# Two transformer blocks on one core: small inputs on another queue, rotary angles and row transposes earlier, the gate columns in another stage

## The reference

```
mod = c @ w_ada + b_ada                       # c is one row: 1024 -> 3 x 1024
shift, scale, gate = split(mod, 3)
h = rmsnorm(x, pre_norm_g) * (1 + scale) + shift
q, k, v, z_ret, u_val, u_gate, z_conv, g_a, g_b = split(h @ w_in)
qh, kh = rotary(q, positions), rotary(k, positions)
y_a = (head_groupnorm(retention(qh, kh, v)) * silu(z_ret)) @ w_ret_out
a = silu(layernorm(causal_depthwise_conv(u_val * sigmoid(u_gate), conv_w) + conv_b))
y_b = (a * silu(z_conv)) @ w_conv_out
y = (sigmoid(g_a) * y_a + sigmoid(g_b) * y_b) @ w_out
x = x + gate * rmsnorm(y, post_norm_g)        # gate is wanted here only
```

## Time and profile before

| | |
|---|---|
| median of three runs | 1937.9 us (1937.62 to 1944.29) |
| profiled execution, its own time | 1937.75 us |
| its span | 1935.9 us, so 1.85 us lie around the span |
| PE busy, mean granted clock | 1719.5 us (89%), 0.943 of full speed |
| DVE, ACT, POOL busy | 1138.3, 893.8, 796.3 us |
| DMA | 357.94 MB, mean 185 GB/s |

### The profile page before, as it was taken

How to read it: one execution, slowest core, us unless ns; L and a number is a source line. 1 busy time by engine, 2 the same in 40 slices (tenths; PEclk the granted TensorE clock), 3 DMA queues, 4 the chain that set the end, 5 groups by cost and what they waited for, 6 DMA issues and landing times.

```text
span 1935.9 us, 22760 instructions
## 1 busy us (share of the span) xinstructions
PE 1719.5 (89%) x7364; PEld 1246.5 (64%) x7364; DVE 1138.3 (59%) x1523; ACT 893.8 (46%) x1196; POOL 796.3 (41%) x388
## 2 busy tenths in 40 slices
PE   1888999989999899989689998873999999999993
PEld 1766878777878688458577467662566656666562
DVE  4667865472232346335553314225899998998995
ACT  3534433443224122123321134331888888888882
POOL 0476977333424144104202031100566556665663
PEclk9899999999999899999859999885999999999997
DMA  8344435222242213412104232122999999999995
GB/s 287 115 121 124 129 118 184 88 97 93 76 147 88 109 40 123 165 66 82 67 1 128 87 131 87 44 87 85 337 395 396 393 389 389 396 391 395 389 370 189
DMA packets 138669, 357.94 MB, mean 185 GB/s; under 512 B 12661, under 2 KB 64125, under 8 KB 113768
## 3 DMA queue, kind: packets, MB, share of 16 engines
q1 hardware_dynamic: 130264, 325.32, 46.1%
q10 hardware_dynamic: 4544, 18.88, 2.5%
q0 software_dynamic: 3792, 12.85, 2.1%
HBM read 333.95 MB, written 23.07 MB: 184 GB/s over the span
## 4 chain that ended last, share of the span: by engine, by line
PE 48%; issue 19%; POOL 14%; DVE 11%; DMA 4%; ACT 2%; SPq 1%; POOLq 0%; DVEq 0%; ACTq 0%
PE ps L720 11%; PE ps L721 11%; PE ps L722 11%; PE ps L692 10%; POOL parts L2284 9%; PE ps L702 3%; POOL idx L2294 2%; DMA ring<-in_w_in 1%; DVE act_parts L1671 1%; POOL parts L2250 1%; PE ps L928 1%; PE ps L901 1%; POOL arena L2297 1%; DMA ring<-in_w_out 1%; DMA arena<-in_sgu_b 1%
## 5 line engine op out<-in xcount | busy, mean ns | idle before, releaser
L2250 POOL TENSOR_TENSOR parts<-ring,parts 128x1024 fp32r<-128x1024 f32 x150 | 371.0, 2480 | 808.1 <-ACT parts L1087 805.3
L1366 ACT CAST parts<-ring 128x1024 fp32r<-128x1024 f32 x384 | 396.2, 1048 | 90.9 <-PE ps L722 67.2
L720 PE MATMUL ps<-parts,act_parts 128*128 128x512 f32 (+2 forms) x1088 | 427.8, 393 | 7.1 <-DVE parts L2074 2.2
L721 PE MATMUL ps<-parts,act_parts 128*128 128x512 f32 (+2 forms) x1088 | 423.7, 389 | 0.0
L722 PE MATMUL ps<-parts,act_parts 128*128 128x512 f32 (+2 forms) x1088 | 423.2, 389 | 0.0
L2074 DVE TENSOR_TENSOR parts<-ring,parts 128x1024 fp32r<-128x1024 f32 x289 | 394.3, 1415 | 26.0 <-ACT parts L1366 19.3
L2284 POOL TENSOR_TENSOR parts<-ring,parts 128x1024 fp32r<-128x1024 f32 x95 | 264.1, 2781 | 235.8 <-ACT parts L1366 235.2
L1087 ACT CAST parts<-ring 128x1024 fp32r<-128x1024 f32 x150 | 155.6, 1047 | 409.4 <-PE ps L722 288.5
L720 PE MATMUL ps<-act_parts,parts 128*128 128x512 f32 x640 | 253.9, 397 | 20.4 <-POOL parts L2250 15.6
L721 PE MATMUL ps<-act_parts,parts 128*128 128x512 f32 x640 | 251.0, 392 | 0.0
L722 PE MATMUL ps<-act_parts,parts 128*128 128x512 f32 x640 | 250.9, 392 | 0.0
(11 more groups left out here) (248 smaller groups left out, 1824.3 us busy)
## 6 DMA issues: line engine op xcount, KB each, us to landing
ring<-in_w SPq DMA_DIRECT2D x192, 1024.0 KB, 7.6
ring<-in_w_in SPq DMA_DIRECT2D x30, 1024.0 KB, 7.3
ring<-in_w_in SPq DMA_DIRECT2D x34, 512.0 KB, 5.6
ring<-in_w_ada SPq DMA_DIRECT2D x12, 1024.0 KB, 11.4
ring<-in_w_ret_out SPq DMA_DIRECT2D x8, 1024.0 KB, 10.8
ring<-in_w_out SPq DMA_DIRECT2D x8, 1024.0 KB, 9.7
y_rows<-arena ACTq DMA_DIRECT2D x32, 256.0 KB, 6.4
ring<-in_w_in SPq DMA_DIRECT2D x16, 256.0 KB, 4.0
```

The source lines that it names most:

```text
L720: pe.matmul(o, lhs[1], rhs[0], start=start, stop=False)
L721: pe.matmul(o, lhs[0], rhs[1], start=False, stop=False)
L1366: act.copy(parts[:, n % 4, 0, :], ring[:, j, n % 4 * 1024:(n % 4 + 1) * 1024]).then_inc(piece_hi, 1)
L2250: pool.tensor_tensor(parts[:, g % 4, 1, :], ring[:, st.place(j), k * 1024:(k + 1) * 1024], parts[:, g % 4, 0, :].bitcast(F32), ALU.subtrac ...
```

## The change

It does these things:

- The positions, the small rows and the conv taps are issued by ACT at its very start, from ACT's queue. SP issues all of `ada` 0 to 3 behind x without them.
- The angle work is DVE's first work; it waits for the constants and the positions.
- On PE, `hT` comes ahead of `columns`.
- The gate's chunks leave the conv loop. In the `mix` stage they pass through slots 1 and 2, between chunks 2 and 3 of the mix; DVE sums them behind the merges of the first third; PE adds them up between the two halves of the last third, and DVE multiplies with `post_norm_g` ahead of the last third's merges. SP loads `post_norm_g` and the bias behind mix chunk 3, when `actT_ready` has reached 24. `conv_use` and `conv_chunk` go, `mix_use` comes, the bank and chunk plans follow.

```diff
@@ plans @@
-    ("columns", 1, 1), ("hT", KT, 1), ("mod", 1, 1), ("conv", [CONV_BANKS[k % 6] for k in range(conv_use(5 * KT))], 1), ("hq0", GROUP_A, 1),
+    ("hT", KT, 1), ("columns", 1, 1), ("mod", (1,), 1), ("conv", [CONV_BANKS[(k + 1) % 6] for k in range(5 * KT)], 1), ("hq0", GROUP_A, 1),
...
-    *[(f"mix{n}", GROUP_A + GROUP_B, 1) for n in range(3)],
+    *[(f"mix{n}", GROUP_A + GROUP_B, 1) for n in range(2)], ("mix2", GROUP_A, 1), ("gate", GROUP_B[2:], 1), ("mix2b", GROUP_B, 1),
...
-    ("ada", 4, 1), ("conv", [(k + 1) % 3 for k in range(3 * KT + 2)], 1), ("hq0", 1, 1), *[(f"head{h}", (1, 2, 0), 1) for h in range(HEADS - 1)],
-    (f"head{HEADS - 1}", (1, 2), 1),
-    ("mix", 6, 1), ("out", 2, 1), ("in2", (2, 0, 1, 0), 1),
+    ("ada", 4, 1), ("conv", [(k + 1) % 3 for k in range(3 * KT)], 1), ("hq0", (1,), 1), *[(f"head{h}", (2, 0, 1), 1) for h in range(HEADS - 1)],
+    (f"head{HEADS - 1}", (2, 0), 1),
+    ("mix", (1, 2, 0), 1), ("gate", (1, 2), 1), ("mix_rest", (0, 1, 2), 1), ("out", 2, 1), ("in2", (2, 0, 1, 0), 1),
...
@@ sync: start @@
             ada("ada", 0, 0)
-            per_feature = [a["conv_w"][0], a["conv_b"], a["conv_ln_g"], a["conv_ln_b"], row(a["norm_mix_2"]),
...
-                sp.dma_start(colrows[at:at + v.shape[0], :], v).then_inc(cols_in, 16)
...
-            sp.dma_start(sgub_rows[:, :], a["sgu_b_2"]).then_inc(cols_in, 16)
             ada("ada", 1, 1)
             ada("ada", 2, 2)
             ada("ada", 3, 3)
-            sp.dma_start(pos_i[:, :], a["positions"].partition_broadcast(P)).then_inc(pos_in, 16)
@@ sync: conv loop @@
-                if t in GATE_AT:
-                    n = GATE_AT.index(t)
-                    ada("conv", GATE_CHUNKS[n], 4 + n)
-                    if n == 0:
-                        sp.wait_ge(rotary_ready, 1)
-                        sp.dma_start(post_g, a["post_norm_g"].partition_broadcast(P)).then_inc(rows_in, 16)
...
@@ sync: mix @@
             mix_gates(0)
+            ada("gate", 0, 4)
+            ada("gate", 1, 5)
             mix_chunk(3)
+            sp.wait_ge(actT_ready, 3 * KT)
+            sp.dma_start(post_g, a["post_norm_g"].partition_broadcast(P)).then_inc(rows_in, 16)
+            sp.dma_start(bada[0:1, :], a["b_ada"][:, 2 * D:]).then_inc(rows_in, 16)
             mix_gates(1)
@@ tensor: start @@
             pe.wait_ge(const_in, 16)
+            pe.wait_ge(h0_ready, MT)
+            for t in range(KT):
+                turn("hT", t, [h0[:, m, t * P:(t + 1) * P] for m in range(MT)])
             pe.wait_ge(cols_in, 16 * 13)
...
-            pe.wait_ge(h0_ready, MT)
-            for t in range(KT):
-                turn("hT", t, [h0[:, m, t * P:(t + 1) * P] for m in range(MT)])
@@ tensor: conv loop @@
-                if n == 5 * GATE_TILE:
-                    pe.wait_ge(rows_in, 32)
-                    for g in range(2):
...
@@ tensor: mix @@
+                    if (n, j) == (2, 1):
+                        pe.wait_ge(rows_in, 32)
+                        for g in range(2):
+                            pe.wait_ge(ada_ready, 5 + g)
+                            filled("gate", g, product(bank("gate", g), [cst("ones"), cst("ones"), cst("ones", 1)],
+                                                      [gate_sum[:, 2 * g, :], gate_sum[:, 2 * g + 1, :],
+                                                       bada[0:1, g * 512:(g + 1) * 512]]))
+                    stage, k = mix_use(n, 4 * j)
@@ scalar: start @@
+            act.dma_start(pos_i[:, :], a["positions"].partition_broadcast(P)).then_inc(pos_in, 16)
...
+                act.dma_start(colrows[at:at + v.shape[0], :], v).then_inc(cols_in, 16)
...
+            act.dma_start(sgub_rows[:, :], a["sgu_b_2"]).then_inc(cols_in, 16)
             act.wait_ge(x_in, 16)
@@ vector: start @@
+            dve.wait_ge(const_in, 16)
+            dve.wait_ge(pos_in, 16)
+            own(dve.tensor_copy(angle, pos_i[:, :]))
...
+            dve.nop().then_inc(angles_ready, 1)
             dve.wait_ge(c_in, 16)
@@ vector: conv loop @@
-                if i in GATE_AT:
-                    n = GATE_AT.index(i)
-                    weigh_rows("conv", GATE_CHUNKS[n], gate_sum[:, 2 * n:2 * n + 2, :])
...
@@ vector: mix @@
+                if n == 0:
+                    for g in range(2):
+                        weigh_rows("gate", g, gate_sum[:, 2 * g:2 * g + 2, :])
+                if n == 1:
+                    for g in range(2):
+                        own(dve.tensor_tensor(gate_post[:, g * 512:(g + 1) * 512], full("gate", g),
+                                              post_g[:, g * 512:(g + 1) * 512], ALU.mult))
+                        own.wait()
+                        drained("gate", g, dve.nop())
```

More of the change, by code:

```diff
@@ L177, with mix_use @@
 MOE_PIECES = [("moe_first", 8, 1), ("moe", 12, 1)]
-GATE_CHUNKS = tuple(3 * i + n for n, i in enumerate(GATE_AT))
-def conv_chunk(j):
-    return j + sum(1 for i in GATE_AT if j >= 3 * i)
+def mix_use(n, k):
+    return ("mix2b", k - 4) if n == 2 and k >= 4 else (f"mix{n}", k)
 def dense_pieces():
@@ L194, in stage @@
         for j, n in enumerate(per_chunk):
-            use = conv_chunk(j) if name == "conv" else j
-            chunk_of.extend((name, use, k, k == n - 1) for k in range(n))
+            use = ("mix_rest", j - 3) if name == "mix" and j >= 3 else (name, j)
+            chunk_of.extend((*use, k, k == n - 1) for k in range(n))
         ends.update({first[name] + p: fill for p, fill in last.items()})
-    stage("conv", (2, 2, 1) * KT, {n: ("conv", conv_use(n)) for n in range(5 * KT)})
+    stage("conv", (2, 2, 1) * KT, {n: ("conv", n) for n in range(5 * KT)})
     stage("hq0", (4,), {3: ("hq0", 3)})
@@ L312, in build @@
         part_b = carve([S])
+        gate_sum = carve([4, S], at=MT * D)
+        post_g, bada = carve([D], at=MT * D + 4 * S), carve([D], at=MT * D + 4 * S + D)
         x = carve([MT, D], at=ARENA - MT * D)
@@ L585, in mix_chunk @@
                 src = (w_ret[:, 0:KT], w_ret[:, KT:], w_conv)[j // 2]
-                chunk("mix", j, lambda r: pair(r, src[:, :, j % 2 * 512:(j % 2 + 1) * 512]))
+                stage, use = ("mix", j) if j < 3 else ("mix_rest", j - 3)
+                chunk(stage, use, lambda r: pair(r, src[:, :, j % 2 * 512:(j % 2 + 1) * 512]))
             def mix_gates(j):
@@ L1572, in _ @@
             for i in range(KT):
-                p = conv_use(5 * i)
-                if i in GATE_AT:
-                    n = GATE_AT.index(i)
-                    weigh_rows("conv", GATE_CHUNKS[n], gate_sum[:, 2 * n:2 * n + 2, :])
-                if i == GATE_TILE:
-                    for g in range(2):
-                        own(dve.tensor_tensor(gate_post[:, g * 512:(g + 1) * 512], full("conv", p - 2 + g),
-                                              post_g[:, g * 512:(g + 1) * 512], ALU.mult))
-                        own.wait()
-                        drained("conv", p - 2 + g, dve.nop())
+                p = 5 * i
                 o = full("conv", p)
```

103 lines of the change are left out of this document (44 added, 59 removed).

## The result

| | median, us | runs, us |
|---|---|---|
| kernel before | 1939.94 | 1937.62 to 1944.29 (5) |
| changed kernel | 1929.09 | 1926.94 to 1929.9 (5) |

The ratio is 0.9941, 95% interval 0.9924 to 0.9958. The profiled execution of the changed kernel took 1926.94 us, with a span of 1925.1 where before it was 1935.9. Forecast was 1911, range 1901 to 1923: the direction was right, the size was not. Of the 26.6 us forecast, 10.8 came.

What follows compares the result with a forecast made beforehand. PE was taken as the bound, busy 89% of the span, losing time at the start and in waits for POOL. 6.4 + 15.6 + 4.0 + 5.9 − 5.3 = 26.6 us off 1937.75 gave 1911.2, said as 1911; range 1901 to 1923.

Steps and rivals of the forecast that it cites:

- The shift: Mix: DVE's two gate sums, 9.9 us, delay the merges and so SP's load of `w_conv_out` by 1.5 us.
- the mix's fourth chunk: Mix: it waits for the third's slot, but its load is there at 705, before PE wants it: no cost.
- the product's +4.0: Mix: PE's gate product, 5.9 us between the last two chunks, makes the out stage start 4.0 us later.
- The start: Before the conv loop: its first matmul comes at 52.1 instead of 58.48, a gain of 6.4 us.
- PE's tail: Start: PE's late transposes (5.55 us) and most `mod` matmuls behind the last `ada` sum move into DVE's time.
- The conv loop: Conv loop to the heads: 15.6 us of PE's waits for POOL, 4 of lower clock and the 5.9 product go.
- Rival 2: First conv tiles: POOL or ACT becomes the limit, half the waits (8 us) stay: 1921 us, chance 0.15.
- All behind the first block runs as before, only sooner: After the first block: no gain or loss of its own, 0 us.
- 1: Start: the two queues overlap, the rows cost nothing, 8.6 us more gained: 1902.5 us, chance 0.13.
- 3: Start: ACT is held at its issues at 2.82 us each, so 6.4 becomes −14.5: 1932 us, chance 0.07.
- 4: Start: each ACT issue ends only when the transfers ahead have drained; slower, up to 1960 us, chance 0.04.
- 5: Start: x is held up more than 8.6 us and the start gains nothing: 1918 us, chance 0.06.

Runs made afterwards that it cites:

- no_low: The changed kernel without POOL's low parts of the mix's weight pieces (24 subtractions left out): 1919.64 us, ratio 0.9882.
- no_sum: The changed kernel with each of DVE's two gate sums in the mix cut to two of its eight terms: 1917.9 us, ratio 0.9885.
- pool_hold: The changed kernel with POOL's first low parts begun only when DVE's fourth `ada` sum is done: 1925.28 us, ratio 0.9924.
- taps_split: The changed kernel with the 31 rows of conv taps loaded in two transfers, of 16 and 15 rows: 1918.97 us, ratio 0.9897.
- rows_sp: The changed kernel with the small rows issued from SP behind its first `ada` chunk, positions still on ACT: 1924.64 us, ratio 0.9910.
- columns_first: The changed kernel with the columns transposed ahead of x again and the bank plan of before: 1932.02 us, ratio 0.9953.
- both: The changed kernel with the taps in two transfers and the first gate sum ahead of the first pair's merges in the mix: 1911.37 us, ratio 0.9853.

## Why the prediction was wrong

- *The failing step*: "The shift is 0.4 to 4.2; I take 1.5, of which PE feels 1.3." It measured 6.8, of which PE felt 6.4, and 2.7 more through the clock. I had the mechanism (an L1506 that meets POOL), but counted two meetings at most, since only the TENSOR_SCALARs have a row with a maximum. The twelve STTs meet POOL just the same (0.74 becomes up to 2.90). In the trace before none of the 36 STTs of the `ada` sums is long (0.75 at most), but another line with two inputs, a merge's multiplication in the mix, is long (2.90 us, the row behind this point), and I passed it over. The right bound was POOL's own count: 4 instructions in the 18 us, so 8.4 us. I also took POOL's beat to be even. ACT now waited 9.36 us for the mix's fourth chunk, which I had called hidden; it was hidden from PE, but its pieces came close together, and so did three of POOL's low parts, in DVE's sums. no_low shows the whole of it: 9.9 us, mix 142.9. The prediction's own sign of this came: from the heads' first matmul to out it took 470.1 us, 13.4 more than the 456.7, where it had put its limit at 8.

```profile
749.10 2.90 DVE L1740 TENSOR_TENSOR arena<-arena 128x512 f32<-128x512 f32 x1
```

- *Right in the mix*: the product's +4.0 (143.1 in no_sum), 12 matmuls of 5.89 us, out without a wait for `w_out`, and that the chain over SP to `w_conv_out` had no slack.
- *The start*, 3.4 for 6.4. Right: ACT's fourteen issues end at 6.2 us, x at 18.1, the sums without a gap, PE's transposes from 29.2. Wrong were three sizes behind the third sum. "four sums of 0.88 + 4.05 = 4.9 us": the fourth took 2.1 more beside POOL, which the change itself had let start 5 us sooner (pool_hold: 4.06). And "only a quarter of the `mod` matmuls is left, 8.83/4 = 2.2 us": the sixteen ran at a clock of 0.50, in 3.57, whether PE had stood ahead of them for 4.75 us or for 1.42 (taps_split). The third, 0.6, is the time from the sum's end to PE's first matmul, which I left out. That is 4.1 us; 1.1 came back, as DVE's first sum began at 24.88 and not at 26.0. That the gain is PE's tail alone, and the rows only move their price, was right: rows_sp and columns_first show it.
- *The conv loop*: 26.2 for 25.5. PE's idle time fell from 17.5 to 1.5 us (15.6 forecast), its busy time by 10.3 (4 and 5.9 forecast). Rival 2 fell: POOL was never waited for, though it works as much as before (194.9 us).
- *"All behind the first block runs as before, only sooner"* was wrong by 5.4 us, of which two executions of each kernel bear out 4.2 to 4.4, the second block's. I know of no row of before that could have shown it, and its cause stays open.
- *Rivals*: 1 is refuted as put (x landed at 18.14, not near 11), though taps_split gets half of its gain by another way. 3 and 4 fall with the issues' end at 6.2 us, and 5 as x was held by 7.4 us and the start did gain. Rival 3's time (1932) was nearest, for a reason that didn't occur.

The forecast of 1911 is what the kernel takes once the sums are moved and the taps are cut (*both*, 1911.37). That is a coincidence of size: it gains 6.5 us more at the start than the changed kernel, by a change to the taps that the forecast didn't have, and still loses 1.5 us in the second block.

## What to carry to other kernels

When work is moved on DVE, count the POOL instructions that run in its new time, and take 2.2 us for each, not the average of before; a late load bunches them. It is the upper end of what was seen here: in taps_split POOL paid instead. A transfer of 31 rows is worth cutting before one changes the queue that issues it. And a new wait of PE can cost more than its length: behind the 5.3 us in the mix PE ran at half speed for 6.3 us. It need not: behind a wait of 3.19 us in the second block of before it ran at 1.00.

## What the hardware did that I had not expected

- Two fp32 TENSOR_TENSORs of DVE, of its share of the mix's left-hand tiles, took 3.3 us beside POOL's subtractions and 1.53 without them (no_low), so the mix pays this price in other places than the sums too. DVE in no_low:

```profile
657.58 1.53 DVE L1647 TENSOR_TENSOR act_parts<-arena,act_parts 128x512 fp32r<-128x512 f32 x2 [3.85 <-ACT act_parts L1157]
```

- 124 KB in one transfer of 31 rows held a 2 MB load back by 4.5 us more than as 16 and 15 rows (18.14 and 13.61). All small rows together with the positions had cost x 7.4 us (10.75 to 18.14). The Trainium skill, "DMA: Bandwidth & Descriptors", section "Why a DMA increments its semaphore by 16 and not by 1", has a transfer run on as many engines as the largest number up to sixteen that divides its outer size: one for 31 rows, sixteen for 16, fifteen for 15. The landing of x agrees with that; the trace was read for the landing alone, not for the engines.
- The granted clock in a stretch of unchanged code was 1.00 in both executions of one kernel and 0.66 in all fourteen others: 1.7 us each time.
